# Score sets and compressed scores spread between the query tiles of the last attention, and the tanh table loaded ahead of the first gate tile

## The reference, cut to what matters

```
gates = sigmoid(gate_logits + b_gate)
merged = gates[0] * proj(o_swa) + gates[1] * proj(o_dsa) + gates[2] * proj(o_mem)
```

```
q     = (h @ w_q) * 64**-0.5          # 16 heads of 64, two heads to a tile of 128 columns
gates = sigmoid(h @ w_g)              # 3 per head: compressed, selected, window
p_c = softmax(q @ k_cmp + bias); p_s = softmax(q @ k_sel + bias); p_w = softmax(q @ k_win + bias)
out = (gates[0]*p_c @ v_cmp + gates[1]*p_s @ v_sel + gates[2]*p_w @ v_win) @ w_o
```

## Time and profile before

| | us |
|---|---|
| median of 3 timed runs | 1367.06 (1366.78 to 1367.82) |
| the profiled execution | 1367.69 |
| its span, first to last instruction | 1366.0 |
| PE busy | 1347.6 (99%) |
| DVE busy | 1048.0 (77%) |
| ACT busy | 651.8 (48%) |
| mean granted clock of PE | 0.997 of full |

### The profile page before, as it was taken

How to read it: one execution, slowest core, us unless ns; L and a number is a source line. 1 busy time by engine, 2 the same in 40 slices (tenths; PEclk the granted TensorE clock), 3 DMA queues, 4 the chain that set the end, 5 groups by cost and what they waited for, 6 DMA issues and landing times.

```text
span 1366.0 us, 22528 instructions
## 1 busy us (share of the span) xinstructions
PE 1347.6 (99%) x8881; PEld 1225.3 (90%) x8881; DVE 1048.0 (77%) x1548; ACT 651.8 (48%) x825; POOL 76.5 (6%) x86
## 2 busy tenths in 40 slices
PE   9999999999999999999999999999999999999997
PEld 7989998898899998999899998989999887899996
DVE  7969697777877778668987778767777867777777
ACT  6565644333443444554353434444343568643432
POOL 2000060000000000100020000100000100200000
PEclk9999999999999999999999999999999999999999
DMA  9533756776657867565566666767566630566661
GB/s 308 185 127 117 239 179 201 242 231 205 213 202 246 274 203 235 186 195 171 167 222 212 202 202 220 250 210 232 199 200 200 186 106 25 183 218 210 201 205 62
DMA packets 191809, 268.70 MB, mean 197 GB/s; under 512 B 5789, under 2 KB 164929, under 8 KB 191472
## 3 DMA queue, kind: packets, MB, share of 16 engines
q1 hardware_dynamic: 186574, 249.95, 56.9%
q0 software_dynamic: 4368, 16.44, 3.6%
q10 hardware_dynamic: 786, 1.18, 0.4%
HBM read 262.32 MB, written 4.19 MB: 195 GB/s over the span
## 4 chain that ended last, share of the span: by engine, by line
PE 91%; DVE 5%; ACT 3%; issue 1%; DMA 0%; DVEq 0%; SPq 0%; ACTq 0%
PE bank L902 88%; PE bank L925 2%; DVE split L2382 1%; ACT arena L2267 1%; ACT split L1865 1%; DVE arena L2620 1%; ACT act_out L2276 0%; DVE best L2619 0%; DVE act_out L2744 0%; DVE gain_rows L2637 0%; ACT xn L2267 0%; ACT gain_rows L2003 0%; DMA resid<-in_x 0%; DVE stats L2436 0%; DVE resid L2431 0%
## 5 line engine op out<-in xcount | busy, mean ns | idle before, releaser
L902 PE MATMUL bank<-hT,split 128*128 128x512 f32 (+2 forms) x4472 | 674.3, 311 | 1.5 <-ACT hT L1887 0.8
L902 PEld LDWEIGHTS bank<-hT,split 128*128 128x128 f32 (+1 forms) x4472 | 623.8, 191 | 47.2 <-issue 4.6
L2382 DVE TENSOR_TENSOR split<-ring,split 128x2048 fp32r<-128x2048 f32 x218 | 496.8, 2281 | 188.7 <-ACT split L1865 185.8
L1865 ACT ACTIVATE split<-ring 128x2048 fp32r<-128x2048 f32 (+1 forms) x220 | 419.7, 1910 | 458.0 <-PE bank L902 443.5
L902 PE MATMUL bank<-split,hid_hi 128*128 128x512 f32 x992 | 271.2, 380 | 2.0 <-DVEq L2805 1.4
L902 PEld LDWEIGHTS bank<-split,hid_hi 128*128 128x128 f32 x992 | 183.2, 189 | 27.2 <-issue 2.4
L902 PE MATMUL bank<-split,hT 128*128 128x256 f32 (+2 forms) x1320 | 172.7, 289 | 1.3 <-DVE split L2422 0.6
L902 PEld LDWEIGHTS bank<-split,hT 128*128 128x128 f32 x1320 | 160.8, 192 | 7.7 <-issue 3.3
L902 PE MATMUL bank<-split,hid_lo 128*128 128x512 f32 x496 | 151.4, 379 | 0.0
L2744 DVE TENSOR_REDUCE act_out<-bank 128x256 f32<-128x512 f32 x188 | 128.6, 686 | 20.3 <-PE bank L902 19.8
L902 PEld LDWEIGHTS bank<-split,hid_lo 128*128 128x128 f32 x496 | 93.8, 189 | 13.2
(11 more groups left out here) (250 smaller groups left out, 884.0 us busy)
## 6 DMA issues: line engine op xcount, KB each, us to landing
ring<-in_ffn_w SPq DMA_DIRECT2D x132, 1024.0 KB, 5.3
ring<-in_w_in SPq DMA_DIRECT2D x17, 1024.0 KB, 5.8
ring<-in_w_mlp_in SPq DMA_DIRECT2D x16, 1024.0 KB, 6.0
ring<-in_w_mlp_out SPq DMA_DIRECT2D x16, 1024.0 KB, 5.1
ring<-in_sgu_w_in SPq DMA_DIRECT2D x16, 1024.0 KB, 5.4
ring<-in_sgu_w_out SPq DMA_DIRECT2D x8, 1024.0 KB, 4.9
ring<-in_kv_w SPq DMA_DIRECT2D x6, 1024.0 KB, 5.5
ring<-in_w_out SPq DMA_DIRECT2D x4, 1024.0 KB, 5.1
```

The lines of the kernel that those rows point to most:

```text
L902: ins = pe.matmul(o, lhsT, rhs, start=start, stop=stop)
L1865: act.activation(halves(q if i is None else q + BODY, n)[0], ring[:, u % SLOTS, 0:n], ACT.Copy).then_inc(hi_ready, 1)
L2382: dve.tensor_tensor(lo, ring[:, u % SLOTS, 0:n], hi.bitcast(F32), ALU.subtract).then_inc(split_ready, 1)
```

## The change

Five edits are made.

1. PE: the two blocks of pair 0 are parted by queries 3, and those of pair 1 by the first half of the compressed scores, queries 5 and the second half. `compressed_scores` takes the blocks to compute; it opens its tile with the first and counts it done with the last. The two blocks of pair 2 are parted by `pair_values(0)`, so that block 1 of pair 2 and block 0 of pair 3 stand next to each other.
2. The list of tiles names `("q", 5)` ahead of `("cs", 0)`, which swaps their two banks.
3. ACT: `pair_exps(0)` and `pair_exps(1)` are split in two; the second half of pair 0 comes after the copy of queries 3, the second half of pair 1 after `compressed_exps(0)` and ahead of `pair_probs(0)`.
4. DVE: block 1 of pair 0 comes after the low part of unit ("q", 3); block 1 of pair 1 comes after `pair_normalize(0)` and `compressed_maxima(0)`.
5. ACT: `load_table(ACT.Tanh)` (one activation on a 128x1 column, L1880) is put in front of `gate(0, 0)`.

```
-    ... [("q", i) for i in range(4)] + [("qt",), ("q", 4), ("cs", 0), ("q", 5)] + probs(0)
+    ... [("q", i) for i in range(4)] + [("qt",), ("q", 4), ("q", 5), ("cs", 0)] + probs(0)
...
-            def compressed_scores(c):
-                for i in range(4 * c, 4 * c + 4):
-                    tile_copied(pe, ("q", i))
-                o = open_tile(("cs", c))
-                for b in range(NB):
+            def compressed_scores(c, blocks=range(NB)):
+                if blocks[0] == 0:
+                    for i in range(4 * c, 4 * c + 4):
+                        tile_copied(pe, ("q", i))
+                    open_tile(("cs", c))
+                o = bank_of(("cs", c))
+                for b in blocks:
...
-                ins.then_inc(tile_done, 1)
+                if blocks[-1] == NB - 1:
+                    ins.then_inc(tile_done, 1)
...
-            for b in range(NB):
-                pair_scores(0, b)
+            pair_scores(0, 0)
             queries(3)
+            pair_scores(0, 1)
             gate_rows()
             queries(4)
-            for b in range(NB):
-                pair_scores(1, b)
-            compressed_scores(0)
+            pair_scores(1, 0)
+            compressed_scores(0, (0,))
             queries(5)
+            compressed_scores(0, (1,))
+            pair_scores(1, 1)
             pair_probs(0)
             queries(6)
             compressed_probs(0)
-            for b in range(NB):
-                pair_scores(2, b)
+            pair_scores(2, 0)
             pe.wait_ge(fills, 5)
             pair_values(0)
+            pair_scores(2, 1)
             pair_scores(3, 0)
             queries(7)
             pair_scores(3, 1)
...
             act.wait_ge(cols_ready, 1)
+            load_table(ACT.Tanh)
             gate(0, 0)
...
-            pair_exps(0)
+            pair_exps(0, (0, 1))
             queries(3)
+            pair_exps(0, (2, 3))
             queries(4)
-            pair_exps(1)
+            pair_exps(1, (0, 1))
             queries(5)
             compressed_exps(0)
+            pair_exps(1, (2, 3))
             pair_probs(0)
...
-            for b in range(NB):
-                pair_maxima(0, b)
+            pair_maxima(0, 0)
             low_unit(("q", 3))
+            pair_maxima(0, 1)
...
-            for b in range(NB):
-                pair_maxima(1, b)
+            pair_maxima(1, 0)
             pair_normalize(0)
             compressed_maxima(0)
+            pair_maxima(1, 1)
             compressed_weights(0)
             pair_normalize(1)
```

More of the change, by code:

```diff
@@ L192, in probs @@
         return [("pt", i, p) for p in range(4)]
-    names += [("qg",)] + [("q", i) for i in range(4)] + [("qt",), ("q", 4), ("cs", 0), ("q", 5)] + probs(0)
+    names += [("qg",)] + [("q", i) for i in range(4)] + [("qt",), ("q", 4), ("q", 5), ("cs", 0)] + probs(0)
     names += [("q", 6), ("ct", 0), ("ov", 0), ("q", 7), ("cs", 1)]
```

## The result

| | before | after |
|---|---|---|
| median of the timed executions | 1367.06 us (1366.29 to 1368.35, 9) | 1370.98 us (1367.41 to 1371.81, 9) |
| profiled execution: time, span | 1367.69, see above | 1367.41, 1365.7 |

The ratio is 1.0023, with a 95% interval of 1.0013 to 1.0033: slower, by just over the 0.2% that can be told from none. The forecast was 1368.4 with a range to 1370.0, so the median lies 1 us outside it.

A forecast was written before the change was run, and what follows sets the result against it. PE, busy 99% of the span, was taken as the bound. Attention +0.6 and table -0.7 gave 1367.6 against the profiled 1367.69; without its 1.48 low clock in most timed executions, 1368.4 was forecast, range 1366.2 to 1370.0.

The forecast's parts named there:

- The table: First gate tile: loading tanh's table early gains 0.7 us, cutting PE's idle 0.93 to about 0.25.
- Queries 6 was to wait 2.25: Ahead of queries 6, PE idles 2.25 us for ACT's first copy of pair 0's turned tiles.
- Pair 2 parted: Values of pair 0 between pair 2's blocks: DVE 1.0 late, the small stall saved returns at block 0 of pair 3.
- The forecast for the profiled execution with the clock held: Whole kernel against the profiled 1367.69: +0.6 for the attention, -0.7 for the table, giving 1367.6.
- The attention was to end 0.6 later: End of the last attention: 0.6 us later than in the profiled execution, though queries 6 starts 0.6 earlier.
- the stall less nothing else: Pair 0 parted on PE by queries 3: pair 1 starts 0.76 us earlier, with no further cost of changing matmul shape.
- DVE's lateness at block 1 of pair 4: Block 1 of pair 4: DVE 0.8 late, against a margin of 0.15, makes PE 0.6 to 0.7 late.
- the first rival: Clock falls behind the 2.25 us idle ahead of queries 6, after turns and small scores; chance 0.25.
- a single fall, of 1.48 at most: Low clock in queries 5 of the profiled kernel before, which took 4.36 us, 1.48 more than 2.88.
- the 1.4 that I forecast: Whole kernel: slower by 1.48 - 0.1 = 1.4 us if most timed executions before lack the clock's fall.
- Two reasons that I gave against the rival: PE's idle 0.93 at the first gate tile left the clock up; the fall followed just one of several alike stretches.
- one accident among several alike places: Last attention: the 1.48 fall followed one stretch, not pairs 0, 2 and 3, so most timed executions lack it.

The follow-up runs named there:

- r2: The kernel before with only the tanh table load put in front of the first gate tile: 1366.16 us, ratio 0.9995.
- r15: The kernel before with only the tanh table load in front of the first gate tile, measured again: 1366.02 us, ratio 0.9992.
- r4: The kernel after with ACT's copies of pair 0's turned tiles ahead of the second half of pair 1's exponentials: 1367.99 us, ratio 1.0010.
- r13: The kernel before with the table load and pair 0 parted on PE, ACT and DVE: 1365.15 us, ratio 0.9981.
- r11: The kernel before with only PE's two blocks of pair 2 parted by the values of pair 0: 1369.51 us, ratio 1.0017.
- r1: The kernel after, unaltered, measured again: 1371.19 us, ratio 1.0034.
- r9: The kernel after, unaltered, measured once more beside its variants on one chip: 1369.41 us, ratio 1.0015.
- r3: The kernel after without the table load: 1371.03 us, ratio 1.0034.
- r12: The kernel after with 16 throw-away matmuls ahead of queries 6 and three ahead of the second compressed scores: 1368.95 us, ratio 1.0008.
- r5: The kernel after with PE's two blocks of pair 2 put back together: 1366.9 us, ratio 0.9994.
- r14: The kernel after with pairs 0 and 2 put back together, leaving the table load and pair 1 parted: 1369.04 us, ratio 1.0011.
- r10: The kernel after with pair 2's blocks put back together, measured again on another chip: 1367.53 us, ratio 1.0002.
- r8: The kernel after with pair 0's copies before pair 1's later exponentials, pair 2 together, first output unit's rounding behind `compressed_probs(0)`: 1367.25 us, ratio 0.9994.
- r6: The kernel after with sixteen throw-away matmuls on PE ahead of queries 6: 1369.51 us, ratio 1.0007.

## Why the prediction was wrong

**Right, with its numbers.** The waits came where the forecast had them, but for one. The table: PE's 0.93 became 0.18 (forecast 0.25), and the rows show 0.75 gained; r2 and r15 measure 0.9995 and 0.9992, that is 0.7 and 1.1 us, intervals that take in no change. Queries 6 was to wait 2.25 for ACT's copy behind `pair_exps(1, (2, 3))`; it waited 2.11, and r4, which moves only that copy, removed it. Pair 2 parted was to bring a wait in block 0 of pair 3 and 0.6 to 0.7 at pair 4: there were 0.65 and 0.81. The forecast for the profiled execution with the clock held was 1367.6; it took 1367.41.

**Right by luck.** The attention was to end 0.6 later than in the profiled execution, and did: 56.37 - 55.78 = 0.59. But two errors of 0.4 cancel in it. Counted from the first scores, queries 6 was to start at 17.90 and started at 17.49 (1113.59 - 1096.10), 1.0 earlier than before and not 0.6. One term of this is pair 0: parting it was to give 0.76, "the stall less nothing else", and gave 0.94 in r13, mostly since block 1 takes 0.97 and not 1.1. Behind queries 6, 1.2 was to be lost and 1.6 was, the price of pair 2 in r11. The start of the attention has little part in it: it came 0.85 earlier than in before, of which the table is 0.75.

**Mis-placed.** I had the last wait in DVE's lateness at block 1 of pair 4. PE meets it earlier, at the second compressed scores, and what it waits for is ACT's copy of queries 7. That copy stands behind ACT's exponentials of block 0 of pair 3, which waited 1.24 for DVE's extremes: DVE's lateness reaches PE through ACT's list. I had looked only for who follows DVE in its own list.

**The step that failed** is the first rival, *the clock falls behind the new wait*: I gave it a chance of 0.25 and reckoned with a single fall, of 1.48 at most. It isn't the exception: all three profiles of after or of after without the table taken later show it (r1, r9, r3), and 17 of 27 timed executions of after have a mean clock of 0.997 or less, against 30 of 116 of before on the four chips of the experiments. And it isn't one fall: the 2.11 and the 0.81 each have their own, 1.64 and 1.29, together 2.93. The forecast had a wait of 0.6 to 0.7 for the second place, but no price of the clock for it. By the same working, an execution with both takes 1367.6 + 2.93 = 1370.5; the profiled ones with both took 1371.21 (r1) and 1370.78 (r9), the median measured was 1370.98, and those of r1 and r9 1371.19 and 1369.41.

A rough estimate of the shift from these rows: the order costs 56.37 - 54.15 = 2.22 against an attention without a fall, the table gives back 0.75, two falls in 17 of 27 executions are 1.84 of mean, and one of 1.48 in 30 of 116 for before is 0.38. That makes 2.22 - 0.75 + 1.84 - 0.38 = 2.93; the three ratios measured, 1.0023, 1.0034 and 1.0015, are 3.1, 4.6 and 2.1 us. Without the falls it would have been near the 1.4 that I forecast. It is rough, since the timed executions give only mean clocks, and a mean of 0.997 or less is neither proof of two falls in the attention nor a mean of 0.998 proof of none.

Two reasons that I gave against the rival didn't hold. PE's idle 0.93 at the first gate tile did not lower the clock (1.00 in every window of before from 66.00 to 80.00), but that is one idle time of less than half the length, with only 1.47 of turns between it and wide work. Ahead of queries 6 stand compressed scores, scores and turns, and PE was busy for 1.29 of 3.40 us in r1's window. And I took the earlier trace rows as one accident among several alike places, where it was a sign that this part of the attention can lose the clock: it lost it there with an idle of only 0.31.

The falls came here behind idle times of 2.11 and even 0.81, with thin matmuls around them, and in the kernel before with none longer than 0.31. In r12, where the 2.11 was filled to 0.32 and the 0.81 in whole, the profile has no fall.

**What stays open.** What decides, from one execution to the next, whether the clock falls at a given place: the rows around 2.11 are the same in the profile of after (none) and in r1 (fall). That filling the gaps did away with the executions of low mean clock is shown. That the gap alone causes the fall isn't: r5, r11 and r14 have such gaps and no fall in their profiles. The medians of r11 and r14, 1369.51 and 1369.04, lie 1.9 and 1.4 above the estimates from their stretches (1311.9 + 55.76 and + 55.75); some executions with falls would make that, but no profile of theirs shows one. r12 is 0.6 above its estimate, which is open, and r9 is only 0.5 above r12, less than falls in 7 of its 12 executions would lead one to expect. And it is open why the start of the run differs, from which the 1 to 2 us between executions at equal mean clock seem to come; in the profiles they do.

## What to carry to other kernels

Spreading small matmuls between wide tiles paid here only where it left the order of work for the engines behind as it was (pair 0). In whole it removed stalls of 0.31 and put in waits of 2.11, 0.65 and 0.81. Ahead of the 2.11 and the 0.81, ACT's copy stood in its list behind exponentials that had been made late (r4, which moved only those of the first place, had no wait ahead of queries 6). Part one block at a time and measure each: one of three parts gained 0.9 and the others lost 1.6 apiece. The falls of the clock behind the new idle times of 2.11 and 0.81 cost 1.64 and 1.29 here, so count a possible fall for each new idle time among thin work, and take it from several executions: the profile of after shows none of it, those of r1 and r9 two. Before comparing profiled times, take off what lies ahead of the change: here it differed by 1.5 us and more between executions, and the forecast's sum and r12's expectation were both measured against a single one.

## What the runs showed of the hardware

- With thin matmuls around it, an idle time of PE of 2.11 (r1, r3, r9, r10), 1.49 (r8) or 0.81 to 0.82 (r1, r4, r6, r9) was followed by a granted clock of 0.50 of full after 1.00, and in after, r5 and r14 (2.11), after and r11 (0.81) it wasn't. A fall in queries 6 cost 1.64 us, and the two in one attention 2.93. Sixteen and three throw-away matmuls in the idle times (r12) left no timed execution under a mean clock of 0.998.
- Whether it falls differs between executions of one unaltered kernel with the same waits to a hundredth: none in the profile of after, two in r1 and in r9.
- The table load took 1.28 in both places, and the activation behind it began 0.02 after its end (65.42 + 1.28 = 66.70, then 66.72): no further cost of the load shows.
- The clock fell near the start of a run too: in r13 a wait of 1.92 for DVE was followed by a granted clock of 0.57 from 30 to 34 us, and of 1.00 from 34 to 40. All that differs between the profiles apart from the changes lies there: the turns ahead of the first gate tile begin from 65.66 to 69.12, and from the ten turns behind the tanh to the attention they run alike to 0.4 us.
